# Expert rows read back and summed while the last expert runs, and the last expert's rows brought to their tokens by TensorE

## The chip, the cores and the metric

The kernel runs on one core of one Trainium2 chip. The metric is the device time of one execution in microseconds (us), the median of several runs. Engines are named TensorE (PE), VectorE (DVE), ScalarE (ACT), GpSimd (POOL) and SyncE (SP); SP does nothing but issue DMAs. PEld is TensorE's loading of weights, PEclk the share of full speed that its clock was granted.

## What is computed

One layer of an encoder over 384 tokens of width 2048: 256 tokens of one new stream (the prompt) and 128 of eight running streams (the samples). First comes a mixer (windowed attention beside gated linear attention), then a mixture of 32 experts, and a final normalization. All is float32. What the change touches is the second half:

```python
h = modulate(rmsnorm(x, g_ffn), sh2, sc2)
# the router picks for every token a group of 8 experts and in it 2 experts, with gates
gates = softmax(top_v) * p_sel
# per expert, over the tokens that chose it
yb = (silu(xblk @ w_eg[e]) * (xblk @ w_eu[e])) @ w_ed[e]
y = segment_sum(yb * slot_w, slot_tok)    # two gated rows per token are summed
x = x + gt2 * y                           # gt2 is one row for the prompt, one per sample stream
y_out = x * rsqrt(mean(x * x) + eps) * g_final
```

## The kernel before

Tokens are held in three tiles of 128 (`t` is 0 and 1 for the prompt, 2 for the samples), rows in partitions: `x[:, t, :]`. Each expert has 64 slots. The router part makes, on the chip, a table of the tokens of each slot; `gtab` and `stab` hold for expert `e` in column `e` the row of the normalized tokens to fetch and the row of the result to write. A row is kept as two halves of 1024 columns, half 0 in partitions 0 to 63 and half 1 in partitions 64 to 127, so that an expert's result is a tile of 128 x 1024.

**The experts.** They run one after the other, `e = 2 * i + u`, in a loop over pairs with the first pair written out (`peeled`, L58). For each expert, TensorE multiplies the slots' rows by the gate and up weights (`up`, L1250: 128 matmuls of 256 columns), transposes the next expert's fetched rows (`rows_T`, L1239), transposes the hidden rows (`hidden_T`, L1265) and multiplies them by the down weights (`down`, L1272: 32 matmuls of 512 columns). DVE and ACT form silu(gate) x up between them (`hidden` L2054, `exp_gate` L1563), and copy the two result banks to `ysb` (L2065, L1576). POOL then issues the scatter of these rows to the DRAM tensor `y_rows` (`scatter`, L635), and the gather of the rows of the expert after next (`gather`, L630).

**The weights.** An expert has 12.6 MB of them. SP issues them as six DMAs of 2 MB each (`expert`, L414) into a ring of 12 units of 1 MB, two units at a time, each as soon as the units' last use by the expert before is counted in `unit_used`. So at most one expert's weights are on their way or waiting.

**Overflow.** Experts with more than 64 tokens get further blocks. Their number `n_over` is computed on the chip and read by every engine into a register behind the last expert (L441, L675, L1300, L1591). With these inputs it is 0, and the branches do nothing. For them POOL scatters the token numbers into a table in DRAM with six indirect DMAs (L652) ahead of the second gather.

**The end.** When the last scatter has landed and `n_over` is known, POOL signals `moe_done` (L692). ACT then issues the three reads of `y_rows` (L1602): for each tile `t` the rows of both choices of each token, 2 MB, into the ring (`yk[t]`). For each tile: ACT multiplies the first choice by its gate (`gated`, L1607), DVE multiplies the second by its gate and adds (L2151), multiplies by gt2 (L2152, `gbc`) and adds to `x` (L2153). ACT squares and sums (L1615) and computes 1/rms (`inv_rms`, L1321 and L1324), and DVE refines it with five small operations (`refine`, L1636 to L1640). The product with 1/rms and `g_final` is made for tiles 0 and 1 by ACT and POOL (L1621, L696), for tile 2 by DVE (L2146). POOL issues the output DMAs (L698).

## Time and profile before

| | |
|---|---|
| time before, median of 3 runs | 1856.45 us (1856.37 to 1859.54) |
| the profiled execution, its own time | 1859.65 us |
| its span in the profile | 1858.0 us |
| PE busy | 1562.1 us, 84% |
| DVE, ACT, POOL busy | 393.5, 201.3, 181.9 us |
| moved by DMA | 610.93 MB, mean 329 GB/s |
| mean granted TensorE clock | 0.942 |
| the chain that ended last | PE 49%, DMA 43%, DVE 3%, the rest under 2% each |

Times within the execution are us from the start of the span. A window row gives, for a stretch, each engine's busy time with its number of instructions, then the granted clock, the mean busy share of the 16 DMA engines, and what they moved. A timeline row has the start, the busy time, the engine, the line and operation, output `<-` inputs, shapes, and how many instructions it merges; in brackets stands the idle time ahead of it and who ended it. A DMA's row on an engine is its issue alone; "to landing" is counted from there. "Issue" in brackets means that nothing the profile shows was waited for.

### The profile page before, as it was taken

The page shows a single profiled execution, that of the slowest core. Times are in us where ns is not written, and L with a number is a line of the kernel's source. Part 1 is how long each engine was busy: PE and PEld are TensorE (multiplying, and loading weights), DVE is VectorE, ACT ScalarE, POOL GpSimd, SP SyncE. Part 2 cuts the span into 40 slices and gives each one's busy share as a digit, 9 for nine tenths or more (in the row PEclk, how much of TensorE's full clock was granted, in tenths as well). Part 3 has the DMA queues.
Part 4 walks back from the last instruction along what each step waited for, and adds up shares of the span by engine and source line. Part 5 has one row for each costly group of instructions (what it writes and reads, how often), then busy time and mean ns, then how long its engine had stood idle before and what let it go on. Part 6 is the DMA issues. An engine that isn't in the chain of part 4 may idle for free.

```text
span 1858.0 us, 21570 instructions
## 1 busy us (share of the span) xinstructions
PE 1562.1 (84%) x8849; PEld 806.4 (43%) x8849; DVE 393.5 (21%) x852; ACT 201.3 (11%) x504; POOL 181.9 (10%) x372
## 2 busy tenths in 40 slices
PE   5999999999999999968798877777787888787840
PEld 2455444444454444554444434444444344444410
DVE  2012322224251311441111111101011111111115
ACT  3001111111221000200000000000000000000013
POOL 1031000000101020031010101010000011010102
PEclk9999999999999999978998999999989899999975
DMA  9998767666514593399999999999999999999952
GB/s 364 375 307 306 283 263 291 268 243 262 181 55 126 177 245 123 157 310 428 425 428 427 427 427 427 428 426 424 426 421 423 422 427 425 426 423 426 419 220 93
DMA packets 101954, 610.93 MB, mean 329 GB/s; under 512 B 15949, under 2 KB 18109, under 8 KB 65929
## 3 DMA queue, kind: packets, MB, share of 16 engines
q1 hardware_dynamic: 84242, 562.29, 74.8%
q0 software_dynamic: 16848, 41.68, 7.4%
q10 hardware_dynamic: 816, 6.29, 0.8%
q8 instruction: 34, 0.56, 0.1%
q14 instruction: 14, 0.11, 0.0%
HBM read 603.03 MB, written 28.40 MB: 340 GB/s over the span
## 4 chain that ended last, share of the span: by engine, by line
PE 49%; DMA 43%; DVE 3%; POOL 1%; issue 1%; ACT 1%; SPq 0%; POOLq 0%; DVEq 0%; ACTq 0%
DMA ring<-in_w_expert_up 36%; PE bank L823 9%; PE bank L1123 7%; PE bank L819 7%; PE bank L1260 6%; DMA zbuf<-h_rows,cur 5%; PE bank L1283 3%; PE bank L777 3%; PE bank L764 3%; PE bank L1150 2%; PE bank L743 1%; PE bank L768 1%; DMA ring<-in_w_ada 1%; DMA ring<-in_w_in 1%; DVE ring L2152 1%
## 5 line engine op out<-in xcount | busy, mean ns | idle before, releaser
L1260 PE MATMUL bank<-ring,zbuf 128*64 128x256 f32 x4096 | 464.2, 383 | 84.2 <-DMA ring<-in_w_expert_up 75.3
L1260 PEld LDWEIGHTS bank<-ring,zbuf 128*64 128x64 f32 x4096 | 291.5, 138 | 264.7 <-DMA ring<-in_w_expert_up 95.8
L1283 PE MATMUL bank<-ring,hbuf 128*64 128x512 f32 x1024 | 269.0, 685 | 17.6 <-ACT hbuf L1573 17.6
L823 PE MATMUL bank<-ring,hbuf 128*128 128x512 f32 x384 | 174.2, 599 | 2.9 <-ACT xbuf L1366 2.6
L1283 PEld LDWEIGHTS bank<-ring,hbuf 128*64 128x64 f32 x1024 | 82.3, 158 | 184.6 <-issue 182.7
L819 PE MATMUL bank<-hbuf,ring 128*128 128x384 f32 x384 | 133.8, 495 | 1.2 <-ACT zbuf L1362 0.8
L1123 PE MATMUL bank<-ring,zbuf 128*128 128x512 f32 x288 | 127.0, 595 | 3.1 <-DVE ring L1881 1.9
L2057 DVE TENSOR_SCALAR hbuf<-hbuf 128x256 f32<-128x256 f32 x32 | 9.4, 294 | 524.7 <-ACT hbuf L1565 524.7
L823 PEld LDWEIGHTS bank<-ring,hbuf 128*128 128x128 f32 x384 | 70.2, 190 | 83.7 <-issue 82.7
L819 PEld LDWEIGHTS bank<-hbuf,ring 128*128 128x128 f32 x384 | 69.8, 190 | 52.5 <-issue 11.0
L641 POOL CAST cur<-stab 128x1 int32 (+1 forms) x32 | 5.8, 181 | 861.5 <-DVE zbuf L2065 861.5
L1243 PE MATMUL bank<-ident,zbuf 128*128 128x128 f32 x264 | 43.2, 313 | 51.4 <-DMA zbuf<-h_rows,cur 51.4
L1123 PEld LDWEIGHTS bank<-ring,zbuf 128*128 128x128 f32 x288 | 53.7, 190 | 68.8 <-issue 68.7
L2065 DVE COPY zbuf<-bank 128x512 f32<-128x512 f32 x32 | 22.1, 692 | 286.8 <-PE bank L1283 286.8
L1565 ACT ACTIVATE hbuf<-bank 128x256 f32<-128x256 f32 x32 | 12.3, 384 | 523.1 <-PE bank L1260 523.1
L1243 PEld LDWEIGHTS bank<-ident,zbuf 128*128 128x128 f32 x264 | 35.2, 198 | 65.2 <-DMA zbuf<-h_rows,cur 60.6
L777 PE MATMUL bank<-ring,dbuf 128*32 128x512 f32 x512 | 59.1, 596 | 0.0
L2058 DVE RECIPROCAL hbuf<-hbuf 128x256 f32<-128x256 f32 x32 | 56.1, 1753 | 1.1
L1269 PE MATMUL bank<-ident,hbuf 128*128 128x128 f32 x64 | 17.9, 369 | 45.1 <-DVE hbuf L2060 45.0
L764 PE MATMUL bank<-hbuf,ring 128*128 128x384 f32 x128 | 50.3, 516 | 3.3 <-DMA ring<-in_w_in 3.3
L1576 ACT COPY zbuf<-bank 128x512 f32<-128x512 f32 x32 | 18.8, 586 | 275.5 <-PE bank L1283 275.5
L743 PE MATMUL bank<-ring,dbuf 128*32 128x512 f32 x256 | 39.3, 690 | 5.5 <-DMA ring<-in_w_ada 4.5
(389 smaller groups left out, 1133.4 us busy)
## 6 DMA issues: line engine op xcount, KB each, us to landing
ring<-in_w_expert_up SPq DMA_DIRECT2D x64, 2048.0 KB, 26.7
ring<-in_w_expert_gate SPq DMA_DIRECT2D x64, 2048.0 KB, 25.3
ring<-in_w_expert_down SPq DMA_DIRECT2D x64, 2048.0 KB, 22.9
ring<-in_w_ada SPq DMA_DIRECT2D x96, 1024.0 KB, 7.7
ring<-in_w_in SPq DMA_DIRECT2D x32, 1024.0 KB, 9.0
ring<-in_w_out SPq DMA_DIRECT2D x16, 1024.0 KB, 5.2
ring<-y_rows ACTq DMA_DIRECT2D x3, 2048.0 KB, 12.2
xbuf<-in_x_prompt SPq DMA_DIRECT2D x4, 1024.0 KB, 5.9
```

Of the source, the lines that this page charges most:

```text
L743: last = mm(bank[7][32 * q:32 * q + 32, :], cT[:, 4 * u + q, :], w[:, q, :], start=(u == 0), stop=(u == 3))
L764: last = mm(bank[c][:, 0:TOK], wq[:, k % 4, c * P:(c + 1) * P], hT[:, k, :], start=(k == 0), stop=(k == KC - 1))
L777: last = mm(bank[b][32 * q:32 * q + 32, :], cT[:, k, :], w[:, q * QN:(q + 1) * QN], start=(k == 0), stop=(k == KC - 1))
L819: last = mm(bank[c][:, 0:TOK], w[:, kk_, c * P:(c + 1) * P], hT[:, k, :], start=(k == 0), stop=(k == KC - 1))
L823: last = mm(bank[t][:, :], hT[:, k, t * P:(t + 1) * P], w[:, kk_, :], start=(k == 0), stop=(k == KC - 1))
L1123: last = mm(bank[3 * (b % 2) + t][:, :], zT[:, k, t * P:(t + 1) * P], w[:, i % 4, :], start=(k == 0), stop=(k == KC - 1))
L1150: last = mm(bank[3 + t][:, :], zT[:, k, t * P:(t + 1) * P], w[:, k % 4, :], start=(k == 0), stop=(k == KC - 1))
L1243: last = tr(bank[c // 4][:, (c % 4) * P:(c % 4 + 1) * P], rows[:, c, :], ident[:, :])
L1260: last = mm(bank[2 + u][64 * q:64 * q + 64, 256 * (j // 4):256 * (j // 4) + 256], xeT[u][:, k % 8, k // 8, :], w[:, kk_, 256 * q:256 * q + ...
L1283: last = mm(bank[5 + n][64 * q:64 * q + 64, :], hidT[u][:, k % 2, k // 2, :], unit(8 + k)[:, 1024 * q + QN * n:1024 * q + QN * n + QN], st ...
L2058: link(v.reciprocal(sg[u], sg[u]))
L2065: cp(ysb[u][:, 0:QN], bank[5][:, :]).then_inc(y_v, 1)
```

## The change

It does five things.

1. `peeled` writes out the last pair of experts too, so that expert 31 can have code of its own; its gather of rows for an expert 32 and its scatter are gone.
2. GpSimd fills `y_rows` with zeros (6.3 MB in rows of 2 KB, early in the mixer), so that the rows of the last expert read as zero.
3. SP issues the three reads of `y_rows` behind the last weights, as the units of the ring come free (`rows_back`). DVE and ACT do tiles 0 and 1's sums with them while expert 31 runs or right behind it (`early_sum`, `early_add`).
4. Expert 31's rows stay in SBUF, once times gt2 for the prompt (`y_prompt`), once plain for the samples. A matrix `hot` (slots x tokens) has the gate of token c in row s where slot s of expert 31 belongs to token c. It is made at expert 0 from a diagonal of the gates (`diag`), their rows (`gate_rows`), a ramp of numbers (`iota_p`) and `slot_pair`. TensorE multiplies `hot` with those rows (`back_to_tokens`), and for tile 2 it adds both choices with the diagonals as weights. DVE adds the banks to `x` in pieces of 512 columns, ACT squares them in pieces, and DVE alone makes the last product, in two halves, each put out by a DMA of SP.
5. POOL's six indirect DMAs of the overflow table are moved into the branch that runs only if `n_over` is above 0.

```diff
-    with eng.Fori(1, times) as i:
+    with eng.Fori(1, times - 1) as i:
         if chain:
             chain.enter(i, per)
         body(i)
         if chain:
-            chain.leave(times)
+            chain.leave(times - 1)
+    body(times - 1)
...
+            def rows_back(t):
+                sp.dma_start(yk[t], y_rows[t]).then_inc(yk_in[t], 16)
+            for t in range(NT):
+                sp.wait_ge(unit_used, U_MOE + UE * (NE - 1) + 2 * t + 2)
+                if t == 0:
+                    sp.wait_ge(sct[0], 16 * 16)
+                    sp.wait_ge(sct[1], 16 * 15)
+                rows_back(t)
...
+            sp.nop().then_inc(y2_rdy, 1)
+            for t in range(NT):
+                for hh in range(2):
+                    c = slice(1024 * hh, 1024 * hh + 1024)
+                    sp.wait_ge(fin_rdy, 2 * t + hh + 1)
+                    sp.dma_start(yout[t][:, c], x[:, t, c]).then_inc(fin_out, 16)
+            sp.wait_ge(fin_out, 32 * NT)
...
+            link(g.memset(zero, 0.0))
+            g.dma_start(y_dram.rearrange("(p n) (b c) -> p (n b) c", p=P, c=QN),
+                        zero.unsqueeze(1).broadcast_to([P, 8 * NT, QN])).then_inc(y_zero, 16)
             pool.wait_ge(unit_used, U_OUT)
...
             pool.wait_ge(logit_ps, NT)
+            g.iota(iota_p, [[1, 2 * TOK]], base=0, channel_multiplier=0,
+                   allow_small_or_imprecise_dtypes=True).then_inc(iota_rdy, 1)
             spread_rows(gbc[:, 0, :], gbc[:, 1, :], 3, gbc_in)
+            for q in range(2):
+                g.dma_start(gate_half[64 * q:64 * q + 64, :],
+                            mod_dram[3, 0:1, 1024 * q:1024 * q + 1024].broadcast_to([64, 1024])).then_inc(gbc_in, 16)
             pool.wait_ge(x1, 6)
             g.dma_start(gfin, A["g_final"].unsqueeze(0).broadcast_to([P, D])).then_inc(gfin_in, 16)
-            pool.wait_ge(slots_init, 16)
-            pool.wait_ge(dest_rdy, 1)
-            for c in range(2 * NT):
-                g.indirect_dma_start(slots_dram, bass.IndirectOffsetOnAxis(dest_i[:, c:c + 1].bitcast(U32), 0),
-                                     tok_i[:, c:c + 1], None).then_inc(slots_set, 16)
+            pool.wait_ge(y_zero, 16)
             pool.wait_ge(tabs, 2)
             def expert_rows(i):
                 for u in range(2):
+                    if isinstance(i, int) and 2 * i + u == NE - 1:
+                        return
...
+            def gate_rows():
+                pe.wait_ge(diag_sb, 1)
+                for q, b in ((0, 3), (1, 7)):
+                    for t in range(NT):
+                        last = mm(bank[b][:, 128 + t * P:256 + t * P], ones[:, :], diag[:, q, t, :], start=True, stop=True)
+                    last.then_inc(rows_ps, 1)
+            def back_to_tokens(t, n, b, more):
+                r = slice(64 * (n // 2), 64 * (n // 2) + 64)
+                src = ysb[1] if t == 2 else y_prompt
+                if more:
+                    for k in range(2):
+                        mm(bank[b][:, :], diag[:, k, t, :], yk[t][:, k, QN * n:QN * n + QN], start=(k == 0), stop=False)
+                return mm(bank[b][:, :], hot[r, t * P:t * P + P], src[r, QN * (n % 2):QN * (n % 2) + QN],
+                          start=not more, stop=True)
             rows_T(0, 0, 16)
...
+                        rows_T(1 - u, e + 1, 16 * i + 16 * (1 + u))
                     hidden_T(u, e)
+                    if isinstance(i, int) and e == 0:
+                        gate_rows()
...
                 pe.nop()
+            pe.wait_ge(last_rdy, 1)
+            for t in range(NT):
+                if t == 2:
+                    pe.wait_ge(y2_rdy, 1)
+                for n in range(4):
+                    if t == 2:
+                        pe.wait_ge(fin_sum, n + 1)
+                    back_to_tokens(t, n, LATE_BANKS[t][n], t == 2).then_inc(late_ps, 1)
...
+            def last_rows(e, block):
+                act.wait_ge(unit_used, U_MOE + UE + e * UE)
+                cp(ysb[1][:, 0:QN], bank[5][:, :]).then_inc(y_a, 1)
+                act.wait_ge(y_v, NE + 2 * block)
+                cp(ysb[1][:, QN:2 * QN], bank[6][:, :]).then_inc(y_a, 1)
...
+                        hidden_copy(u, e)
+                        gated(0)
+                        act.wait_ge(sct[1], 16 * 15)
+                        last_rows(e, 0)
+                        gated(1)
+                    else:
+                        rows_copy(1 - u, e + 1)
...
+            def late_squares(t):
+                for n in range(4):
+                    act.wait_ge(fin_sum, 4 * t + n + 1)
+                    act.wait_ge(x1sq, 12 + 4 * t + n)
+                    af(sqf[:, 0:QN], x[:, t, QN * n:QN * n + QN], ACT.Square, accum_out=x1_parts[:, t, n:n + 1]).then_inc(x1sq, 1)
+            late_squares(0)
+            late_squares(1)
+            inv_rms(x1sum, 4, slice(0, 1), slice(0, 1), D)
+            inv_rms(x1sum, 5, slice(1, 2), slice(1, 2), D)
+            late_squares(2)
+            inv_rms(x1sum, 6, slice(2, 3), slice(2, 3), D)
...
-            dve.wait_ge(count_ps, 1)
+            d = ident[:, :].unsqueeze(1).unsqueeze(1).broadcast_to([P, 2, NT, P])
...
+            def slot_gates():
+                link(stt(hot2, iota_p, slot_pair[:, 0:1], gate_row, ALU.is_equal, ALU.mult))
+                tt(hot, hot2[:, 0:TOK], hot2[:, TOK:2 * TOK], ALU.add).then_inc(hot_rdy, 1)
+            def last_rows(e, block):
+                dve.wait_ge(unit_used, U_MOE + UE + e * UE)
+                tt(y_prompt[:, QN:2 * QN], bank[6][:, :], gate_half[:, QN:2 * QN], ALU.mult).then_inc(y_v, 1)
+                dve.wait_ge(y_a, NE + 2 * block)
+                tt(y_prompt[:, 0:QN], bank[5][:, :], gate_half[:, 0:QN], ALU.mult).then_inc(y_v, 1)
+            def early_sum(t):
+                y0, y1 = yk[t][:, 0, :], yk[t][:, 1, :]
+                dve.wait_ge(y_gated, t + 1)
+                link(stt(y0, y1, gate[:, 1, t:t + 1], y0, ALU.mult, ALU.add))
+            def early_add(t):
+                y0 = yk[t][:, 0, :]
+                link(tt(y0, y0, gbc[:, 0, :], ALU.mult))
+                tt(x[:, t, :], x[:, t, :], y0, ALU.add).then_inc(early, 1)
...
+                xs = x[:, t, QN * n:QN * n + QN]
+                if t < 2:
+                    return tt(xs, xs, bank[b][:, :], ALU.add)
+                chain(tt(late_tmp[n], bank[b][:, :], gbc[:, 1, QN * n:QN * n + QN], ALU.mult))
+                return tt(xs, xs, late_tmp[n], ALU.add)
...
-                    rows_copy(1 - u, e + 1)
-                    y_copy(u, e, 16 * i)
...
+                        early_sum(0)
+                        early_add(0)
+                        dve.wait_ge(sct[0], 16 * 16)
+                        last_rows(e, 0)
+                    else:
+                        rows_copy(1 - u, e + 1)
+                        y_copy(u, e, 16 * i)
...
+            def add_late(t):
+                if t < 2:
+                    dve.wait_ge(early, t + 1)
+                for n in range(4):
+                    dve.wait_ge(late_ps, 4 * t + n + 1)
+                    add_rows(t, n, LATE_BANKS[t][n], fin).then_inc(fin_sum, 1)
+            def squares_sum(t):
+                dve.wait_ge(x1sq, 16 + 4 * t)
+                v.tensor_reduce(stat[:, t:t + 1], x1_parts[:, t, :], AX.X, ALU.add).then_inc(x1sum, 1)
...
                 refine(t + 11, slice(t, t + 1), slice(t, t + 1), D)
...
-            for t in range(NT):
...
+                    stt(x[:, t, c], x[:, t, c], rs[:, 0, t:t + 1], gfin[:, c], ALU.mult, ALU.mult).then_inc(fin_rdy, 1)
+            add_late(0)
+            add_late(1)
+            squares_sum(0)
+            squares_sum(1)
+            normed(0)
+            normed(1)
+            add_late(2)
+            squares_sum(2)
+            normed(2)
```

**On POOL, ahead of the second gather.** Before, behind the first gather (L594 are the copies of gt2 per sample stream, L649 is g_final, L641 to L632 the second gather):

```order
L592 DMA dbuf<-mod_rows 128x2048 [waits logit_ps]
L594 DMA dbuf<-mod_rows 16x2048 x8
L649 DMA hbuf<-in_g_final 128x2048 [waits x1]
L653 DMA slot_table<-tok_i,dest_i 12416x1 [waits dest_rdy,slots_init]
L653 DMA slot_table<-tok_i,dest_i 12416x1 x5
L641 CAST cur<-gtab 128x1 [waits tabs]
L628 TENSOR_TENSOR stat<-stat 1x1 [waits ch_p]
L632 DMA zbuf<-h_rows,cur 128x1024
```

and in the changed kernel:

```order
L688 IOTA modr 128x768 [waits logit_ps]
L630 DMA dbuf<-mod_rows 128x2048
L632 DMA dbuf<-mod_rows 16x2048 x8
L692 DMA hbuf<-mod_rows 64x1024 x2
L695 DMA hbuf<-in_g_final 128x2048 [waits x1]
L682 CAST cur<-gtab 128x1 [waits tabs,y_zero]
L669 TENSOR_TENSOR stat<-stat 1x1 [waits ch_p]
L673 DMA zbuf<-h_rows,cur 128x1024
```

The six DMAs to `slot_table` are gone from here, a ramp and two small DMAs (`gate_half`, the L692 row) are added, and the gather waits for `y_zero`.

**On SP, from the last weights on.** In the changed kernel the loop's loads are followed by the reads, on the same queue; before, nothing followed on SP, and the reads stood on ACT behind `moe_done`:

```order
L444 DMA ring<-in_w_expert_down 128x4096 [waits unit_used]
L442 REGISTER_ALU
L444 DMA ring<-in_w_expert_down 128x4096 [waits unit_used]
L452 REGISTER_ALU
L452 COMPARE_AND_BRANCH
L457 DMA ring<-y_rows 128x2x2048 [waits sct1,sct0,unit_used]
L457 DMA ring<-y_rows 128x2x2048 [waits unit_used] x2
L468 TENSOR_LOAD ov_i [waits ov_rdy]
L468 ISA x2
L470 COMPARE_AND_BRANCH [waits yk_in2]
```

The first of the three waits for the scatters of experts 30 and 29 and for units 0 and 1 of expert 31, the others for further units.

**On DVE, the end.** Before, behind the branch, three operations for each tile (L2151 to L2153), here those of tile 2, and the refinement of tile 1's 1/rms:

```order
L2151 SCALAR_TENSOR_TENSOR ring<-ring,gate 128x2048 [waits ch_r,y_gated]
L2152 TENSOR_TENSOR ring<-ring,dbuf 128x2048 [waits ev_v]
L2153 TENSOR_TENSOR xbuf<-xbuf,ring 128x2048 [waits ev_v]
L1636 TENSOR_SCALAR rs<-stat 128x1 [waits rstd]
L1637 TENSOR_TENSOR rs<-rs 128x1 [waits ch_r]
L1638 TENSOR_TENSOR rs<-rs 128x1 [waits ch_r]
L1639 TENSOR_SCALAR rs<-rs 128x1 [waits ch_r]
L1640 TENSOR_TENSOR rs<-rs 128x1 [waits ch_r]
```

and in the changed kernel from expert 31's silu (L2159 to L2162) on, up to the branch:

```order
L2159 TENSOR_SCALAR hbuf<-hbuf 128x256 [waits gu_exp]
L2160 RECIPROCAL hbuf<-hbuf 128x256 [waits ch_v]
L2161 TENSOR_TENSOR hbuf<-hbuf,bank 128x256 [waits ch_v]
L2162 TENSOR_TENSOR hbuf<-hbuf,bank 128x256 [waits ch_v]
L2227 SCALAR_TENSOR_TENSOR ring<-ring,gate 128x2048 [waits y_gated,gbc_in]
L2232 TENSOR_TENSOR ring<-ring,dbuf 128x2048 [waits ch_v]
L2233 TENSOR_TENSOR xbuf<-xbuf,ring 128x2048 [waits ch_v]
L2219 TENSOR_TENSOR zbuf<-bank,hbuf 128x512 [waits unit_used,sct0]
L2221 TENSOR_TENSOR zbuf<-bank,hbuf 128x512 [waits y_a]
L2268 TENSOR_LOAD ov_i [waits ov_rdy]
L2268 ISA x2
```

Tile 0's sum (L2227 to L2233) now stands ahead of the two products that empty expert 31's banks (L2219, L2221). Tile 1's follows the branch. Last of all, tile 2 is added in four pairs (L2242, L2243), and its 1/rms follows from the pieces' squares (L2323, L1737 on). This is the last pair and what is behind it:

```order
L2242 TENSOR_TENSOR zbuf<-bank,dbuf 128x512 [waits late_ps]
L2243 TENSOR_TENSOR xbuf<-xbuf,zbuf 128x512 [waits ev_v]
L2323 TENSOR_REDUCE stat<-stat 128x1 [waits x1sq]
L1737 TENSOR_SCALAR rs<-stat 128x1 [waits rstd]
L1738 TENSOR_TENSOR rs<-rs 128x1 [waits ch_r]
L1739 TENSOR_TENSOR rs<-rs 128x1 [waits ch_r]
```

Behind the branch, where three operations of 2048 columns stood for each tile, tile 0 has now four of 512 columns, tile 1 three of 2048 and four of 512, tile 2 eight of 512.

## Rows read from the trace of the kernel before

**Rows 1.** The chain that ended last, the end (start us, us, what).

```profile
1745.98 27.81 DMA ring<-in_w_expert_up
...
1782.26 9.70 PE bank L1283 x32
...
1793.60 2.94 DMA y_rows<-zbuf,cur
...
1797.77 7.70 DMA ring<-y_rows
```

**Rows 2.** Windows: engines busy, then TensorE's clock, DMA share, GB/s.

```profile
560.00:590.00 30.00, 30.00 (x109) 13.83 (x108) 4.03 (x16) 3.46 (x11) 0.00 (x0) 1.00 0.26 78
816.00:834.00 18.00, 16.55 (x130) 10.37 (x128) 7.97 (x35) 0.97 (x2) 6.07 (x8) 0.85 1.00 217
834.00:850.00 16.00, 11.50 (x60) 5.32 (x62) 4.08 (x6) 1.45 (x3) 0.57 (x3) 0.89 1.01 430
1776.00:1782.00 6.00, 3.31 (x24) 2.01 (x20) 3.49 (x5) 1.21 (x3) 0.00 (x0) 0.89 0.44 186
1782.00:1788.00 6.00, 5.74 (x16) 1.80 (x18) 0.00 (x0) 0.13 (x1) 0.00 (x0) 0.54 0.02 8
1848.00:1858.00 10.00, 0.00 (x0) 0.00 (x0) 0.00 (x0) 0.00 (x0) 0.00 (x0) 0.50 0.00 0
```

**Rows 3.** DMA issues between 1755 and 1763 us (median us to landing).

```profile
ring<-in_w_expert_down SPq DMA_DIRECT2D x2, 2048.0 KB, 24.1
y_rows<-zbuf,cur POOLq DMA_INDIRECT x1, 10.2
```

**Rows 4.** Timeline of the end (start us, us, engine, line, operation).

```profile
1791.98 0.69 DVE L2065 COPY zbuf<-bank 128x512 f32<-128x512 f32 x1 [10.41 <-PE bank L1283]
...
1805.50 2.00 ACT L1607 ACTIVATE ring<-ring,gate 128x2048 f32<-128x2048 f32 x1 [12.93 <-DMA ring<-y_rows]
1807.64 2.35 DVE L2151 SCALAR_TENSOR_TENSOR ring<-ring,gate 128x2048 f32<-128x2048 f32 x1 [14.97 <-ACT ring L1607]
1810.03 2.29 DVE L2152 TENSOR_TENSOR ring<-ring,dbuf 128x2048 f32<-128x2048 f32 x1
...
1824.58 4.67 POOL L696 TENSOR_TENSOR xbuf<-xbuf,hbuf 128x2048 f32<-128x2048 f32 x1 [29.97 <-ACT xbuf L1621]
1824.92 6.48 DVE L2152 TENSOR_TENSOR ring<-ring,dbuf 128x2048 f32<-128x2048 f32 x1
...
1833.64 0.15 DVE L1636 TENSOR_SCALAR rs<-stat 128x1 f32<-128x1 f32 x1
...
1838.58 0.30 ACT L1321 ACTIVATE rs<-stat 128x1 f32<-128x1 f32 x1
...
1841.87 2.35 DVE L2146 SCALAR_TENSOR_TENSOR xbuf<-xbuf,rs,hbuf 128x2048 f32<-128x2048 f32 x1
1844.54 0.53 POOL L698 DMA_DIRECT2D out_y_sample<-xbuf  x1 [2.19 <-DVE xbuf L2146]
```

**Rows 5.** Timeline: GpSimd's copy of gate 1, a ScalarE square, expert 0.

```profile
593.27 0.76 POOL L592 DMA_DIRECT2D hbuf<-mod_rows  x1 [35.90 <-PE bank L823]
...
786.64 0.63 ACT L1521 ACTIVATE hbuf<-xbuf 128x512 f32<-128x512 f32 x1
...
813.95 1.05 POOL L653 DMA_INDIRECT slot_table<-tok_i,dest_i  x1 [0.30 <-issue]
...
817.19 16.16 PE L1260 MATMUL bank<-ring,zbuf 128*64 128x256 f32 x128 [0.80 <-DVE zbuf L2052]
```

**Rows 6.** Timeline: experts 0 and 1, from 822 us on.

```profile
822.48 1.07 POOL L632 DMA_INDIRECT zbuf<-h_rows,cur  x1 [0.16 <-issue]
...
837.97 1.53 PE L1243 MATMUL bank<-ident,zbuf 128*128 128x128 f32 x8 [4.63 <-DMA zbuf<-h_rows,cur]
...
840.45 7.84 PE L1283 MATMUL bank<-ring,hbuf 128*64 128x512 f32 x32 [0.52 <-ACT hbuf L1573]
...
848.13 13.98 PE L1260 MATMUL bank<-ring,zbuf 128*64 128x256 f32 x128
```

## What the change will do to the time

> **What bounds the kernel now.** I read the chain that ended last first, to see where time can be won at all. Up to 1782 us it is pairs of "27 us of a weight load, then 3.7 us of matmuls" [rows 1]: the experts are bound by the bytes of their weights. The windows say the same: from 834 us on the DMA engines are busy all the time and move 430 GB/s [rows 2]. Work of PE, DVE or ACT inside that phase is worth nothing unless it delays a load. Then I read the end of the chain as a list of waits in series. The last down product runs from 1782.26 for 9.70 us, to 1791.96; its scatter lands at 1796.54; the first read of `y_rows` is issued at 1797.77 and takes 7.70 us [rows 1]. From 1805.50 on DVE is the engine that works without a break, for tiles 0, 1 and 2 in turn, and its last product ends at 1844.22 [rows 4]. So 52 us lie between the last matmul and the last arithmetic, and the DMA engines, which held the phase before, have nothing left by 1782 (a busy share of 0.02) [rows 2]. 1844.54 to 1858 are the output DMA and an end in which nothing moves for 10 us [rows 2, 4]; that stays.
>
> I make the sum on the profiled execution (span 1858.0, its time 1859.65, 3.2 above the median of 1856.45), and then take the difference off the median.
>
> **The new end, step by step.** (a) When does `yk[0]` land? The reads stand on SP's queue behind the last two down loads, which take 24.1 us to land; the scatter of expert 30 that the first read waits for is issued in the same window, 1755 to 1763, and takes 10.2 us [rows 3], so the read is issued between 1765 and 1773. The window 1776 to 1782 has the engines 0.44 busy, and then they stop [rows 2]: some of the 16 still have weights until 1782. A load of the kernel lands 27.8 us after its issue though 2 MB need 2.10/0.430 = 4.9 us [rows 1, 2], which is a queue drained in order. I take that: the slowest engine turns to `yk[0]` at 1782.2 and lands it at 1787.1, tile 1's at 1792, tile 2's at 1797. The other bound is that the half-idle engines carry the read alone: 7.70 us after the issue [rows 1], by 1781.
>
> The Trainium skill (DMA: Bandwidth & Descriptors, Queues, rings and completion order) says that on each engine descriptors are consumed in ring order, and that a DMA counts as landed only when all its engines have written. By that rule `yk[0]` can't come before 1787; by the free share of the row alone it would come by 1781, and the end would be 4 us earlier. The rule speaks against part of the gain, and no row here shows two kinds of DMA on that queue.
>
> (b) ACT multiplies it by its gate, 2.00, to 1789.1; DVE's three operations are 2.35 + 2.29 + 2.29 [rows 4], with gaps to 1796.2. (c) In DVE's order the emptying of expert 31's banks comes behind this: the down product ends at 1792 and waits 4 us, but the alternative order would only swap the two. Two products of 512 columns at 0.69 [rows 4] give 1797.6. (d) The branch: from the landed scatter at 1796.54 to ACT's issue at 1797.77 it cost 1.2 us before [rows 1]; so 1798.8. (e) ACT gates tile 1 from 1797.6 to 1799.6, behind its last bank copy; DVE's three operations, 6.95 with gaps, end at 1806.6. (f) TensorE has from 1798.8 on to do eight matmuls of 512 columns with full-width results. Half-width ones took 9.70/32 = 0.30 each in a stretch whose clock was partly 0.54 [rows 1, 2]; twice that is 0.6, and even 0.9 makes 7.2 us, so they end by 1806: hidden, with nothing to spare. Tile 2's twelve (11 us at 0.9) run from 1807 to 1818 under DVE's other work. (g) Eight additions of 512 columns on DVE, 0.72 each with the gap: 1812.4. ACT squares each piece, 0.63 [rows 5] and some 0.25 for the sum's read-out and gaps, so it trails: eight from 1807.4 end at 1814.4. (h) A small sum, and ACT's two functions (0.30 for the first [rows 4], 0.6 for both with gaps), 1815.2. Refinement: five small operations, of which one takes 0.15 [rows 4] and 0.19 with the gap, 0.95; the product over 2048 columns 2.35 [rows 4], in halves 2.4. Tile 0 is ready at 1818.6, tile 1 at 1821.9. (i) Tile 2: eight operations at 0.72, 1827.7; the last square 0.9, sum 0.2, functions 0.6, refinement 0.95, product 2.4: 1832.8. That is 11.4 us before 1844.22. Part of it, 4.2 us, is one row: DVE's product at 1824.92 took 6.48 where the others take 2.29, because it starts beside POOL's 4.67 us product [rows 4], and POOL has none at the end any more. (j) Output: before, DVE's end to the last byte was 1844.22 to 1848 [rows 2, 4], 3.8. Now half of the tile is 1.2 us ahead and SP issues it: 2.6. The end gains 11.4 + 1.2 = 12.6 us.
>
> **The front.** POOL's six indirect DMAs go: from 813.95 to 822.48 the second gather stood behind them, and it took until 837.97 for TensorE to transpose what it brought [rows 5, 6]. Expert 0's up product is not affected (817.19 + 16.16 = 833.35 [rows 5]); its silu takes 3.5 us more, so down could have started at some 838.0 and not at 840.45 [rows 6]. In place of the six there are a ramp and two DMAs, at most 2.5 us, so the gather goes 6 us earlier and is in time. `gate_rows` puts six small matmuls ahead of down, into the 0.52 us in which TensorE waited for ACT anyway [rows 6]: below nothing, 0; above, 8 matmuls of that size took 1.53 [rows 6], so 0.6 of it shows. 2.4 - 0.6 = 1.8 us. Between 816 and 834 us the DMA engines were fully busy at 217 GB/s, half of the 430 behind it [rows 2]: 768 four-byte writes of the table are in there. With a clean queue expert 1's loads come up to 4 us earlier, but the ring frees units only as TensorE uses them, so the gain of the bytes is bounded by TensorE's: I take 2.0, from 0 to 4. The gather and the scatter that fall away at the end are small parts of the traffic: 0.5. So the weights end 2.5 us earlier, and all of the new end with them.
>
> **Edits costed at nothing.** The zero fill is 6.29 MB, 14.6 us at 430 GB/s and 29 at the 217 of small rows [rows 2]. It is issued where POOL begins to wait for gate 1's copies, 35.90 us ahead of 593.27, at 557.4 [rows 5]; from 560 to 590 the DMA engines are 0.26 busy [rows 2], which leaves 22 us, and TensorE has a ring of four units ahead. Without that cover it costs up to 15 us. The next on POOL's queue is the copy of gate 1 at 593.27 [rows 5], which is read only behind the output projection's matmuls. `diag`, 768 columns on DVE (about 0.9), delays `n_over`, which is read first by down of expert 0 at 840.45 [rows 6]. `hot` (some 1.5 us on DVE) and the two row copies on ACT lie under expert 1's up product, 13.98 us [rows 6]. The written-out last pair: expert 0's and 1's are written out too, and expert 1's 128 matmuls took 13.98 us, 0.109 each [rows 6], full speed; bounds 0 and 3 us.
>
> Sum: 12.6 + 2.5 = 15.1 off; 1856.45 - 15.1 = 1841.3, said as 1841.5.
>
> **The rivals.** (A) The forecast, 1837 to 1846: chance 0.57. (B) The read is carried by the free engines, or the front gives 4: the down product then bounds the new end (DVE empties the banks at 1793.4), 4 us better: 1837, with both 1835. The half-idle window speaks for it, the 27.8 us landings against it. 0.13. (C) A wait takes the removed one's place: SP's reads share the engines with the last down load, or the new code is fetched late, or DVE waits for TensorE at step (f) at a slow clock. 6.3 MB more are 14.6 us of traffic; if a third falls ahead of the weights, down ends 5 us later, one of which is hidden by step (c)'s 4: with smaller waits 4 to 9 us worse, 1846 to 1851. 0.18. (D) The change moves work without gain: DVE does as much arithmetic as before, 7 us of it for each tile, and if `yk[0]` only landed at 1800 (its queue blocked), everything follows 13 us later: 1854 to 1857. Against it: the queue is empty at 1782. 0.06. (E) Slower: the zero fill holds back the mixer's loads and the copies of gate 1 behind it on the queue. It decides from the point at which the fill takes more than the 22 free us and TensorE's next unit is late; to be slower than before it must cost over 15 us, all of the 14.6 of its bytes and the slow rows' surplus: 1860. 0.06.
>
> **The numbers.** A measurement of this kernel tells about 0.2% (3.7 us) from no change. Faster by over 0.2% are A, B, C and a little of D: 0.90; same 0.04; slower 0.06. The range takes A and B whole and C up to 1850: 1833 to 1850.
>
> **What would show it.** Step (a): the landing of the first `y_rows` read, 5 us behind the last weight. (b), (c): DVE's three 2048-column operations end after down does. (f): DVE's first addition of 512 columns is not ended by PE. (i): no DVE row of 6.48. Front: TensorE's transposes for expert 1 directly behind its up product, and down of expert 0 at 838 or 839. Wrong it would be if the last weights landed later than 1782, if DVE waited for a read, or if TensorE waited for a load between 560 and 600.

## The result, and the profile after

| | changed | before, same chip and session |
|---|---|---|
| median of the runs, us | 1837.52 (5 runs, 1835.9 to 1845.1) | 1858.87 (5 runs, 1856.37 to 1859.54) |
| profiled execution: span / its time, us | 1835.9 / 1837.52 | 1858.0 / 1859.65 |
| ratio of the times | 0.9895, 95% interval 0.9872 to 0.9917 | |

The kernel is 1.0% faster. The forecast was 1841.5, in a range of 1833 to 1850: the range holds it, but the span fell by 22.1 us (the medians by 21.4) where the sum said 15.1. Start with VectorE (DVE) at the end of the changed kernel, in order of time; the first columns are start and duration, the bracket says how long the engine stood idle and what ended it.

```profile
1791.05 2.35 DVE L2227 SCALAR_TENSOR_TENSOR ring<-ring,gate 128x2048 f32<-128x2048 f32 x1 [9.90 <-ACT ring L1660]
...
1797.97 0.68 DVE L2219 TENSOR_TENSOR zbuf<-bank,hbuf 128x512 f32<-128x512 f32 x1
...
1800.00 0.15 DVE L2304 COPY stat<-stat 128x1 f32<-128x1 f32 x1 [0.75 <-ACT zbuf L1667]
1801.20 2.35 DVE L2227 SCALAR_TENSOR_TENSOR ring<-ring,gate 128x2048 f32<-128x2048 f32 x1 [1.05 <-ACT ring L1660]
...
1808.12 4.86 DVE L2241 TENSOR_TENSOR xbuf<-xbuf,bank 128x512 f32<-128x512 f32 x8
...
1815.29 0.16 DVE L2323 TENSOR_REDUCE stat<-stat 128x1 f32<-128x4 f32 x1 [2.23 <-ACT ring L1715]
...
1816.66 2.48 DVE L2330 SCALAR_TENSOR_TENSOR xbuf<-xbuf,rs,hbuf 128x1024 f32<-128x1024 f32 x2
...
1822.41 0.68 DVE L2242 TENSOR_TENSOR zbuf<-bank,dbuf 128x512 f32<-128x512 f32 x1
...
1830.30 2.48 DVE L2330 SCALAR_TENSOR_TENSOR xbuf<-xbuf,rs,hbuf 128x1024 f32<-128x1024 f32 x2
```

The last down product began at 1782.18, within 0.1 us of before [rows 1]. DVE now ends at 1832.78 where it ended at 1844.22 [rows 4], and no product of 6.48 us is left. That is 11.4 us, as forecast. But the span ends 3.1 us behind DVE, where it ended 13.8 behind. The rows of the kernel's last line, by which an engine leaves the program, say why; their columns are count, min/median/max in ns, and the start of the first and the last. First the kernel before, then the changed one.

```profile
L103 POOLq DRAIN  x1: 8972/8972/8972, 1848.8 to 1848.8; - x1
L103 POOLq EVENT_SEMAPHORE  x2: 17/17/17, 1857.9 to 1857.9; - x2
```

```profile
L104 POOLq DRAIN  x1: 8646/8646/8646, 1774.8 to 1774.8; - x1
L104 SPq DRAIN  x1: 13/13/13, 1835.7 to 1835.7; - x1
L104 POOLq EVENT_SEMAPHORE  x2: 17/17/17, 1835.7 to 1835.8; - x2
```

The stretch "in which nothing moves for 10 us" of the prediction was GpSimd's own way out: a drain of 8.97 us that could start only when the outputs, which GpSimd issued and waited for, had landed. In the changed kernel SP issues the outputs, GpSimd is done at 1774.8, and its drain of 8.65 us lies under the last expert; SP's takes 0.01.

The ledger of the profiled executions: way from the first up product's start to the last down product's, 965.07 before (817.19 to 1782.26) and 962.63 after (819.55 to 1782.18), -2.4; from there to DVE's end 61.96 and 50.60, -11.4; from DVE's end to the span's, 13.78 and 3.12, -10.7; and +2.4 ahead of the experts, together -22.1. The +2.4 isn't shown to be a cost of the change: over the 14 profiles of this study, the first up product starts between 815.8 and 819.7, on the mean at 817.6 in the four without the change and at 818.2 in the ten with it.

The front, in the changed kernel: TensorE, then GpSimd, in order of time.

```profile
819.55 15.73 PE L1298 MATMUL bank<-ring,zbuf 128*64 128x256 f32 x128 [0.80 <-DVE zbuf L2154]
839.63 1.68 PE L1281 MATMUL bank<-ident,zbuf 128*128 128x128 f32 x8 [4.36 <-DMA zbuf<-h_rows,cur]
841.11 0.63 PE L1307 MATMUL bank<-ident,hbuf 128*128 128x128 f32 x2
841.53 2.45 PE L1331 MATMUL bank<-modr,ones 128*128 128x128 f32 x12
843.91 4.51 PE L1321 MATMUL bank<-ring,hbuf 128*64 128x512 f32 x20
```

```profile
809.93 1.11 POOL L673 DMA_INDIRECT zbuf<-h_rows,cur  x1 [0.36 <-issue]
811.06 0.81 POOL L688 IOTA modr<- 128x768 f32 x1
...
818.50 1.07 POOL L673 DMA_INDIRECT zbuf<-h_rows,cur  x1 [0.17 <-issue]
```

The second gather is issued at 818.50, 1.05 us ahead of the up product's start; before it was 5.29 behind it [rows 5, 6], so it went 6.3 us earlier. But it takes 21.1 us to reach TensorE (15.5 before), which waits 4.36 us for it. It isn't chance of this profile: in all ten profiles of the changed kernel and its variants TensorE waits for this gather, 1.4 to 12.1 us, and of the four without the change only in the kernel before (4.63). The down product begins 24.4 us behind the up product's start; before it was 23.3. TensorE got later, and still the weights ended earlier, counted from the up product's start.

### The profile page after: what moved, and what is told of

Its sections match the earlier page's. It is cut to its first block and busy times, and to the rows that moved or that the text cites. A ratio compares the mean times of both kernels' runs of the same rounds, so it can differ in the third digit from the quotient of the medians.

```text
span 1835.9 us, 21665 instructions
## 1 busy us (share of the span) xinstructions
PE 1576.8 (86%) x8893; PEld 815.0 (44%) x8893; DVE 398.2 (22%) x878; ACT 198.7 (11%) x521; POOL 166.1 (9%) x360
## 5 line engine op out<-in xcount | busy, mean ns | idle before, releaser
L1321 PE MATMUL bank<-ring,hbuf 128*64 128x512 f32 x1024 | 260.9, 668 | 16.8 <-ACT hbuf L1672 16.8
L1161 PE MATMUL bank<-ring,zbuf 128*128 128x512 f32 x288 | 128.7, 602 | 3.1 <-DVE ring L1982 1.8
L2159 DVE TENSOR_SCALAR hbuf<-hbuf 128x256 f32<-128x256 f32 x32 | 9.4, 294 | 527.1 <-ACT hbuf L1642 527.1
L2167 DVE COPY zbuf<-bank 128x512 f32<-128x512 f32 x31 | 21.4, 691 | 270.3 <-PE bank L1321 270.3
L815 PE MATMUL bank<-ring,dbuf 128*32 128x512 f32 x512 | 59.1, 596 | 0.0
L1188 PE MATMUL bank<-ring,zbuf 128*128 128x512 f32 x96 | 43.4, 610 | 0.0
## 6 DMA issues: line engine op xcount, KB each, us to landing
ring<-in_w_expert_down SPq DMA_DIRECT2D x64, 2048.0 KB, 23.2
```

The costliest lines, as they stand in the source:

```text
L815: last = mm(bank[b][32 * q:32 * q + 32, :], cT[:, k, :], w[:, q * QN:(q + 1) * QN], start=(k == 0), stop=(k == KC - 1))
L1161: last = mm(bank[3 * (b % 2) + t][:, :], zT[:, k, t * P:(t + 1) * P], w[:, i % 4, :], start=(k == 0), stop=(k == KC - 1))
L1188: last = mm(bank[3 + t][:, :], zT[:, k, t * P:(t + 1) * P], w[:, k % 4, :], start=(k == 0), stop=(k == KC - 1))
L1321: last = mm(bank[5 + n][64 * q:64 * q + 64, :], hidT[u][:, k % 2, k // 2, :], unit(8 + k)[:, 1024 * q + QN * n:1024 * q + QN * n + QN], st ...
L2167: cp(ysb[u][:, 0:QN], bank[5][:, :]).then_inc(y_v, 1)
```

## The experiments

Two lengths are taken from every profile below: the **way**, from the start of the first expert's up product to the start of the last expert's down product, and the **tail**, from there to the end of the span. What varies ahead of the experts is in neither. Before: 965.1 and 75.7. Changed: 962.6 and 53.7.

**pool_stays.** GpSimd leaves only with the outputs.

```diff
             pool.wait_ge(kv_out, 64)
+            pool.wait_ge(fin_out, 32 * NT)
```

> The changed kernel with one wait more: GpSimd waits for all six output DMAs before it ends. In the trace of the kernel before, GpSimd's last instruction is a drain of 8.97 us that starts at 1848.8, behind the last output, and the end of the span follows it; in the changed kernel it takes 8.65 us from 1774.8 on, beside other work. Theory 1 (the drain is what the end of the kernel before was made of): about 9 us longer than the changed kernel, a span near 1845, the drain on the end again. Theory 2 (the old end belongs to DMAs that GpSimd issues): SyncE still issues the outputs here, so no change, within 2 us of the changed kernel.

Measured 1843.02 us, ratio 0.9903 (0.9886 to 0.9921), way 962.8, tail 62.4: the tail is 8.7 longer for one wait. Its rows of the last line:

```profile
L104 POOLq DRAIN  x1: 8646/8646/8646, 1835.4 to 1835.4; - x1
L104 SPq EVENT_SEMAPHORE  x1: 17/17/17, 1844.2 to 1844.2; - x1
```

So the cause of the shorter end behind DVE is shown by these rows: the same drain, moved behind the outputs, is back on the path. The times alone would not show it: the unedited changed kernel didn't run in this group, and its ratio in the first group, 0.9895, lies inside this interval (in the two later groups it was 0.9885 and 0.9868, just below it).

**sp_out.** The kernel before, with its outputs issued and waited for by SP and nothing else changed.

```diff
-                g.dma_start(yout[t], x[:, t, :]).then_inc(fin_out, 16)
-            pool.wait_ge(fin_out, 16 * NT)
+                sp.dma_start(yout[t], x[:, t, :]).then_inc(fin_out, 16)   # on SP
+            sp.wait_ge(fin_out, 16 * NT)
```

> The kernel before with the three output DMAs issued by SyncE, which also waits for them; GpSimd ends behind its product for tile 1 at about 1841. Theory 1 (the drain): GpSimd drains from 1841.3 to 1850.3 beside DVE's last product and the last DMA, so the span ends at about 1850.5, 7 to 8 us less than before. Theory 2 (the end is a fixed cost of any kernel's last DMA): at most 1 us less, what the faster issue brings.

Measured 1852.41 us, ratio 0.9957 (0.9943 to 0.9971), way 967.1, tail 67.1, which is 8.6 less than before. The last line's rows:

```profile
L103 POOLq DRAIN  x1: 13399/13399/13399, 1840.2 to 1840.2; - x1
...
L103 SPq DRAIN  x1: 13/13/13, 1851.6 to 1851.6; - x1
L103 SPq EVENT_SEMAPHORE  x1: 17/17/17, 1853.8 to 1853.8; - x1
```

So this part of the gain can be had without the rest: 7.7 us by the medians of the group (1860.09 to 1852.41). The drain's row has 13.4 us here and ends 2 us behind SP's. Its first part is GpSimd's own product for tile 1, which the edit no longer waits for ahead of the drain:

```profile
1840.07 4.50 POOL L702 TENSOR_TENSOR xbuf<-xbuf,hbuf 128x2048 f32<-128x2048 f32 x1 [7.48 <-ACT xbuf L1624]
```

The product ends at 1844.57, and from there to the drain's end at 1853.6 it is 9.0 us, as in the kernel before. What is left of the drain on the path are those 2 us.

**slots_branch.** The kernel before, with its six indirect DMAs (the slot table) issued only in the branch for overflow, as the change has them.

```diff
-            for c in range(2 * NT):
-                g.indirect_dma_start(slots_dram, ...).then_inc(slots_set, 16)
             ...
             with pool.If(n_over > 0):
+                for c in range(2 * NT):
+                    g.indirect_dma_start(slots_dram, ...).then_inc(slots_set, 16)
```

> The kernel before with the six indirect DMAs of the overflow table moved into the branch, and nothing else changed (the work that these DMAs do is left out at n_over = 0, where nothing reads it). Theory 1 (they cost the expert phase DMA time): the way from the start of expert 0's up product to the start of expert 31's down product, 965.1 us before and 962.6 in the changed kernel, becomes about 962 to 963. Theory 2 (the phase is shorter in the changed kernel because the gather for an expert 32 is gone): this way stays at 965. By TensorE's side (my prediction): its transposes for expert 1 come directly behind expert 0's up product, 2.4 us earlier than before.

Measured 1855.26 us, ratio 0.9974 (0.9962 to 0.9986), 4.8 us under the kernel before of the same group; way 961.4, tail 75.7. The transposes come straight behind the up product, and the DMA engines move 335 GB/s from 816 to 836 us where the kernel before moved 240:

```profile
815.86 16.04 PE L1260 MATMUL bank<-ring,zbuf 128*64 128x256 f32 x128 [0.80 <-DVE zbuf L2052]
831.83 1.16 PE L1243 MATMUL bank<-ident,zbuf 128*128 128x128 f32 x8
835.41 0.51 PE L1269 MATMUL bank<-ident,hbuf 128*128 128x128 f32 x2 [2.41 <-DVE hbuf L2060]
```

**slots_front.** The reverse: the changed kernel with the six DMAs back ahead of the second gather (the same lines, moved the other way).

> The changed kernel with the six indirect DMAs of the overflow table back ahead of the second gather. Theory 1 (their four-byte writes cost the expert phase DMA time): the way from expert 0's up product to expert 31's down product grows from 962.6 to about 966 and the time by 3 us. Theory 2 (the phase is shorter for another reason, the gather for expert 32 or chance): stays within 1 us of 962.6.

Measured 1842.17 us, ratio 0.991 (0.9894 to 0.9925), way 970.2, tail 53.7. TensorE waits 12.1 us for the gather:

```profile
845.12 1.97 PE L1283 MATMUL bank<-ident,zbuf 128*128 128x128 f32 x8 [12.11 <-DMA zbuf<-h_rows,cur]
```

The table costs the changed kernel 7.5 us of way, twice the 3.7 that it costs the kernel before, and 5.6 us by the medians of the group (changed_again: 1836.61). The theory that it costs the expert phase DMA time was right, its 3 us too small.

This kernel and the kernel before both have the table in front, and slots_front has the longer way, 970.2 against 965.1; its time less its tail is 4.5 us longer too. So what else the change puts into the front (the ramp and the copies ahead of the gather, `diag`, `gate_rows`) costs some 4 to 5 us in this pair. Which of them does wasn't tried.

**pair_out.** The kernel before with the last pair of experts written out behind the loop.

```diff
-    with eng.Fori(1, times) as i:
+    with eng.Fori(1, times - 1) as i:
         ...
+    body(times - 1)
```

> The kernel before with the last pair of experts written out behind the loop. Theory 1: nothing, within 0.1%; expert 30 and 31's matmuls as before. Theory 2 (new code is fetched late while the DMA engines are full): TensorE pauses at the loop's end, 1 to 3 us longer.

Measured 1860.7 us, ratio 1.0004 (0.9993 to 1.0014): nothing. It gave something else. Its gather was in time, as in sp_out (TensorE transposed at 833.9, its down product began at 838.4, 2 us earlier than before), and the way was 966.7, no shorter. So the start of the down product alone is not what sets the way. The bytes that have come in its first 40 us go closely with it. This table counts, from the windows of each profile, what the DMA engines moved in the first 40 us of the way (two windows of 20 us; rate times length):

```
kernel             GB/s in each   MB    way, us
slots_front         247  339     11.7   970.2
changed, 3rd time   284  359     12.9   968.3
sp_out              228  427     13.1   967.1
pair_out            228  429     13.1   966.7
before              257  427     13.7   965.1
reordered           320  426     14.9   963.0
pool_stays          322  426     15.0   962.8
banks_first         326  428     15.1   962.3
changed             339  423     15.2   962.6
slots_branch        335  428     15.3   961.4
fill_twice          341  424     15.3   962.2
changed, 2nd time   342  427     15.4   961.8
reordered_banks     343  426     15.4   961.4
reads_act           344  426     15.4   961.7
```

From end to end, 3.7 MB more go with a way that is 8.5 us shorter, 2.3 us for each MB, and 1 MB at the 0.427 MB/us of the full rate is 2.3 us. That is a balance of bytes: what did not come early comes later. Two windows show the table's part of it, of slots_front and of the changed kernel (busy time of each engine, then PEclk, DMA share and GB/s):

```profile
816.00:836.00 20.00, 16.45 (x128) 10.61 (x128) 11.14 (x38) 0.85 (x2) 7.69 (x9) 0.84 1.01 241
```

```profile
816.00:836.00 20.00, 17.70 (x136) 11.73 (x136) 8.73 (x36) 0.97 (x2) 3.31 (x7) 0.82 1.03 324
```

Both keep the DMA engines busy all the time; one of them with 768 writes of four bytes. (The way starts at 816.6 in the first and at 819.6 in the second; the table counts from there.) The second 20 us show another way to lose bytes: in slots_front and in the third profile of the changed kernel, where the gather is latest, the DMA engines are 0.83 and 0.89 busy there and move 339 and 359 GB/s. TensorE, which waits, frees no units of the ring, so there the late down product does hold back the loads.

**changed_again, changed_third.** The changed kernel as it is, in the other two groups of runs.

> The changed kernel, unedited, on the chip and beside the kernel before of the three that follow, as their measure. It should be at 0.989 of the kernel before; from expert 0's up product to expert 31's down product 962 to 963 us, and from there to the end of the span 54 us.

> The changed kernel as it is, for the comparison with the others of this group: 1836 to 1839 us, a ratio to the kernel before of 0.988 to 0.990, and 53.5 to 53.7 us from the start of the last expert's down product to the end.

Measured 1836.61 (0.9885, 0.987 to 0.99), tail 53.5; and 1835.67 (0.9868, 0.9851 to 0.9884), tail 53.4. The third ratio is a little below the 0.988 to 0.990 that was expected. The profiled one of the third group was its longest, 1842.58: GpSimd issued the second gather 2.3 us behind the up product's start, where it was 1.05 ahead in the first profile, TensorE waited 9.63 us for it, and the way was 968.3. Of the changed kernel's 13 runs one in each group stood 4 to 7 us above the next (1845.1, 1841.35, 1842.58); that all three are late gathers is possible, but seen in one profile only.

**fill_twice.** The changed kernel with its zero fill (6.3 MB) issued twice in series.

```diff
+            for _ in range(2):
                 g.dma_start(y_dram..., zero...).then_inc(y_zero, 16)
+                pool.wait_ge(y_zero, 16 + 16 * _)
```

> The changed kernel with its 6.3 MB zero fill issued twice, the second after the first has landed (12.6 MB in all, GpSimd waiting for both). Theory, the fill is hidden: the stretch from 560 to 605 us has the DMA engines' spare time for it, TensorE waits for no load there, the time stays within 0.15% of the changed kernel's, and the way from the first expert's up product to the last expert's down product stays at 961.7 to 962.8 us. Rival, the fill is paid for: the second one delays loads or GpSimd's copies of the gates, and the start of the first expert's up product moves from about 816 to 819 us later by up to 15 us; then a single fill costs some part of that too.

Measured 1834.5 us (1832.81 to 1834.6), ratio 0.9865 (0.9849 to 0.9881), beside 0.9868 for the changed kernel in the same group. The window behind the fill's issue, in the changed kernel and then with the fill doubled, and GpSimd's queue there:

```profile
560.00:590.00 30.00, 30.00 (x109) 13.81 (x108) 3.22 (x13) 3.09 (x9) 0.00 (x0) 1.00 0.75 284
```

```profile
560.00:590.00 30.00, 30.00 (x109) 13.91 (x108) 2.73 (x10) 3.09 (x9) 1.39 (x1) 1.00 0.91 350
```

```profile
580.37 1.39 POOL L637 DMA_DIRECT2D y_rows<-modr  x1 [22.19 <-DMA y_rows<-modr]
606.52 0.78 POOL L630 DMA_DIRECT2D hbuf<-mod_rows  x1 [24.76 <-DMA y_rows<-modr]
```

TensorE is busy for all 30 us in both, and the copies of gate 1 behind the second fill are 14 us late without anyone waiting. The second fill costs nothing that these runs can tell, so the first is unlikely to. A kernel without it wasn't tried.

**banks_first.** The changed kernel, where DVE empties the last down product's banks before it sums tile 0.

```diff
-                        early_sum(0)
-                        early_add(0)
                         dve.wait_ge(sct[0], 16 * 16)
                         last_rows(e, 0)
+                        early_sum(0)
+                        early_add(0)
```

> The changed kernel with DVE's two products that empty expert 31's banks ahead of tile 0's sum (my step (c) took the order for indifferent). In its trace the down product ends at 1790.9 and tile 0's first choice is gated at 1790.94, so the products fit in front and everything behind the branch starts earlier, and ScalarE gates tile 1 while DVE sums tile 0. Theory 1 (DVE is the bound, with its wait of 1.05 us for the gating and 0.75 for the branch): 1.9 us shorter behind the down product, 52 instead of 54. Theory 2 (the order is indifferent): 0.

Measured 1832.88 us, ratio 0.9859 (0.9844 to 0.9874), way 962.3, tail 52.6. Its DVE rows:

```profile
1787.78 0.69 DVE L2219 TENSOR_TENSOR zbuf<-bank,hbuf 128x512 f32<-128x512 f32 x1 [10.86 <-PE bank L1321]
...
1788.99 2.35 DVE L2227 SCALAR_TENSOR_TENSOR ring<-ring,gate 128x2048 f32<-128x2048 f32 x1
...
1795.96 2.34 DVE L2227 SCALAR_TENSOR_TENSOR ring<-ring,gate 128x2048 f32<-128x2048 f32 x1
```

The two waits of 0.75 and 1.05 are gone; 0.9 to 1.1 us of tail remain of it, about half of what was expected.

**reads_act.** The changed kernel with the three reads of `y_rows` on ScalarE's DMA queue, clear of the weights.

```diff
-                rows_back(t)                                              # on SP
+                nc.scalar.dma_start(yk[t], y_rows[t]).then_inc(yk_in[t], 16)
```

> The changed kernel with the three reads of y_rows issued by ScalarE on its own queue, ahead of its exponential for expert 31, at the same time as before (about 1773 to 1775), and no longer behind the weights on SyncE's. Theory 1 (on SyncE's queue the slowest engine turns to the read only behind the weights; a second queue shares each engine): the first read lands earlier than 15.5 us after its issue, at 8 to 12, and the last down weights later, by up to 5 us, so that the down product may wait. Theory 2 (the order of the queue doesn't matter, the engines serve what is there): the landing as now, 15 us.

Measured 1838.79 us, ratio 0.9888 (0.9868 to 0.9908), way 961.7. The first read was issued at 1768.88 and ScalarE's gate product began at 1784.74, 15.8 us later; on SP's queue it was 15.5 in the changed kernel (1773.43 to 1788.93) and 15.0 in changed_again. Measured from the last down product's start it is 6.5 here, 6.8 in the changed kernel:

```profile
1784.74 2.00 ACT L1653 ACTIVATE ring<-ring,gate 128x2048 f32<-128x2048 f32 x1 [6.50 <-DMA ring<-y_rows]
```

```profile
1788.93 2.00 ACT L1660 ACTIVATE ring<-ring,gate 128x2048 f32<-128x2048 f32 x1 [6.81 <-DMA ring<-y_rows]
```

Its own queue didn't bring the read home earlier, and the weights beside it came later: the last expert's two down loads took 25.8 us to land (median), 22.1 in changed_again. Neither theory held whole. The five times are spread from 1832.93 to 1844.19, so the median says little about a gain or a loss.

**reordered, reordered_banks.** Behind the branch, tile 2 first: TensorE multiplies its read-back rows by the gates' diagonals while it waits for the last expert's sums, DVE adds and normalizes in the order 2, 0, 1. The second has banks_first's edit too.

```diff
+            pe.wait_ge(y2_rdy, 1)
+            for n in range(4):
+                for k in range(2):
+                    mm(bank[n][:, :], diag[:, k, 2, :], yk[2][:, k, ...], start=(k == 0), stop=False)
...
-            add_late(0)
-            add_late(1)
-            squares_sum(0)
+            add_late(0, 2)
+            add_late(1, 0)
+            squares_sum(0, 2)
+            normed(0, 2)
```

> The changed kernel with tile 2 first behind the branch: TensorE multiplies tile 2's rows that were read back by the diagonals of the gates before the last expert's sums are ready, where it stood idle in the changed kernel, and VectorE adds in the order 2, 0, 1 with each norm as soon as its squares are there; the outputs leave in that order. Theory, the end is a chain of VectorE's adds with a wait for ScalarE's squares (2.23 us) and tile 2's twelve matmuls in it: about 3.5 us less than the 53.5 to 53.7 us from the last down product's start to the end, 0.2% of the time. Rival, tile 2's rows are read back too late for this (they land last of the three), VectorE waits for TensorE in their place, and the end stays as long as it is.

> The order 2, 0, 1 behind the branch, and the order of the kernel banks_first before it (VectorE empties the last down product's banks before it starts tile 0's sum, which saved 0.9 us there). Theory, the two lie in different parts of VectorE's chain and add up: 4.4 us less than the changed kernel's 53.6, so about 49.2 us from the last down product's start to the end, a time of 1831 to 1834 us, the shortest of this study. Rival: with the banks emptied early the rows of tile 2 are what the end waits for, and the two together give no more than one of them, 50 us or more.

Measured 1834.56 us, ratio 0.9866 (0.985 to 0.9883), tail 52.1; and 1832.53 us, ratio 0.9857 (0.9841 to 0.9874), tail 52.3. The rival of both had the wait right: DVE waits for TensorE, 1.3 us in reordered and 3.3 in reordered_banks. In reordered 1.4 us of the 3.5 remain all the same; in reordered_banks the tail is above 50 us, as the rival said. TensorE and DVE in reordered_banks:

```profile
1797.83 9.31 PE L1382 MATMUL bank<-ring,modr 128*128 128x512 f32 x16 [8.19 <-SPq L483]
```

```profile
1808.31 0.69 DVE L2244 TENSOR_TENSOR zbuf<-bank,dbuf 128x512 f32<-128x512 f32 x1 [3.34 <-PE bank L1386]
```

```profile
1798.00:1803.00 5.00, 5.00 (x7) 2.07 (x8) 4.93 (x4) 0.00 (x0) 0.00 (x0) 0.57 0.01 2
```

SP signals tile 2's rows at 1797.8 (it waited for their landing), so TensorE was idle 8.2 us and began at a granted clock of 0.57, near its lower level of 1.2 GHz; DVE then waited 3.3 us for it. The two edits together gain no more tail than either alone. banks_first and reordered_banks stand lowest, some 3 to 4 us under the changed kernel of their groups, of which the tails explain 1; the intervals overlap, so they are not shown to beat it, only the kernel before.

## Why the prediction was right, and where it was not

**What bounds the kernel**: right. Over 14 profiles the way follows the bytes of its first 40 us, whatever held them back.

**(a) the landing of `yk[0]`**: taken for 1787.1; ScalarE's product began at 1788.93, 1.8 later. The other bound, 1781 on free engines, is out, though the free engines did begin early: 404 GB/s moved from 1776 to 1782, where it was 186, and 426 from 1782 to 1788, where it was 8 [rows 2].

```profile
1776.00:1782.00 6.00, 2.21 (x18) 1.18 (x14) 2.89 (x4) 0.63 (x2) 0.00 (x0) 1.00 0.98 404
1782.00:1788.00 6.00, 5.82 (x20) 1.85 (x22) 0.00 (x0) 0.13 (x1) 0.00 (x0) 0.72 1.01 426
```

The reason given, a queue drained in order behind the weights, isn't borne out: on another queue it took as long (reads_act). The rule of the Trainium skill (DMA: Bandwidth & Descriptors, Queues, rings and completion order), that each engine consumes the descriptors of a ring in order, may well hold, but the order behind the weights isn't needed for this landing. What does set it stays open. The rows show that the DMA engines had no time free from 1776 to 1788.

**(b), (d) to (i)**: right, each end within 2 us. Tile 1's sum ended at 1808.1 (1806.6 in the sum), the eight additions at 1813.0 (1812.4), tile 0 was ready at 1819.1 (1818.6), tile 1 at 1822.4 (1821.9), DVE ended at 1832.8 (1832.8). That the end agrees to 0.1 us is partly luck: 0.9 of the 1.8 us of (a) were given back by additions of 0.61 each where 0.72 was taken, 0.4 by tile 2's eight operations, the rest by small differences. TensorE's eight matmuls ended at 1806.9, hidden with 1.2 us to spare.

**(c) "would only swap the two"**: wrong, by about 1 us. Emptied late, the banks bring ScalarE's copy and its second gate product late as well; banks_first shows it.

**(j) and "an end in which nothing moves for 10 us; that stays"**: this is the step that failed. The working asked what moved in those 10 us and found nothing, but not whose they were. 9.0 us were GpSimd's drain, and the change takes GpSimd off the outputs. The output itself gained 1.7 (from 13.78 - 8.97 = 4.8 to 3.1) where 1.2 was said. Together 10.7 us stand where the sum had 1.2.

**The front, 2.5 us**: the direction was right in the profiles, the mechanism half wrong. "The gather goes 6 us earlier and is in time": it went 6.3 earlier, counted from the up product's start, and was 0.7 earlier at TensorE. "The gain of the bytes is bounded by TensorE's": not here. TensorE started down no earlier, yet 1.6 MB more had come by 40 us into the way, worth some 1.6 / 0.427 = 3.7 us, an estimate. Between the two profiles the way shrank by 2.4, which is the 2.5 of the sum, but not by its reasons. Over the profiles it is 965.1, 966.7 and 967.1 for the kernel before with its table in front, and 961.4 to 963.0 for the changed one and its variants, if changed_third (968.3) and slots_front are left out. The times leave less. In the three groups the changed kernel is 21.4, 23.1 and 22.6 us faster by the medians, and the shorter tails are 22.0 to 22.3 of that. So the whole front, with what varies ahead of the experts, gave between -0.7 and +0.9 us, with an uncertainty of 3 to 4 in each group. The table out of the front is worth about 5 (slots_branch 4.8, slots_front 5.6 by the times); the additions to the front seem to take most of it back. The sum left them at nothing, but for 0.6.

**Costed at nothing**: a second zero fill and the written-out pair cost nothing measurable (fill_twice, pair_out). `gate_rows` was said to show 0.6 us, as six small matmuls. The trace has 12 of them ahead of down, and they took 2.45 us (1.50 in changed_again).

**The rivals**: A (1837 to 1846) held by 0.5 us, and partly by luck: the gain was 6 us above the sum, and the kernel before stood at 1858.87 in this group and not at the 1856.45 from which the sum starts. The two repeats, at 1836.61 and 1835.67, lie just outside A and inside the range. B's price, 1837, was met, but by the drain and not by its cause. The losses of C, D and E didn't happen as a whole; of C's waits, TensorE at a slow clock in (f) was there (a granted clock of 0.50 from 1798 to 1803) and stayed hidden.

## What to carry to other kernels

When a trace ends in a stretch where nothing is busy, ask which engine's last instruction fills it before calling it fixed: let the engine with a slow way out finish early, and give the last DMAs to one that leaves at once. Where a phase is bound by bytes, judge a stray DMA by the bytes that don't move while it is served, not by who waits for it. Check a gain at the front against the times and not only against two profiles, since what is added there can take it back. And a read that is to hide under the last weights shares their engines: here it could be used 6.4 to 6.8 us behind the last down product's start, on either queue.

## What the hardware showed that was not expected

GpSimd's drain at the end of the program took 8.65 to 9.05 us in all profiles (in sp_out counted from the end of GpSimd's last product), also where GpSimd had nothing left to do; SP's took 0.01 to 0.05 and ScalarE's 0.23. A drain's row can also hold what its engine hasn't finished: sp_out's 13.4 us begin beside GpSimd's last product, and TensorE's drain in the changed kernel, 8.99 us from 1813.6 on, ends with its last matmul at 1822.5. With six indirect DMAs of 128 four-byte writes each in front, the DMA engines moved 228 to 257 GB/s over 20 us at a busy share of 0.88 to 1.01, against 320 to 344 GB/s without them (284 in one profile), though the six carry 3 KB. The second gather was transposed 15.5 us behind its issue in the kernel before, at most 11.0 in pair_out and sp_out, 21.1 in the changed kernel and 23.2 in changed_third, the same instruction with the same rows. Why isn't settled.
